# Moving the weight ring's two tiles by 32 bytes in SBUF

## The chip, the core and the metric

The kernel runs on one core of one Trainium2 chip. The metric is the device time of one execution in microseconds (us), the median of several runs. TensorE has two clock levels, 1.2 and 2.4 GHz; in the stretches used below the granted clock is 1.00 of the higher one.

## What is computed

Two transformer blocks of two layers each, all in float32, on a batch of one. The first runs over 16 meta tokens and 256 tokens (272 columns in the kernel), the second over the 256 tokens alone. Cut to what matters here:

```
# block one, twice
h = h + mixer(rms_norm(h), w_in, w_branch, w_out, ...)     # retention, hgrn2, differential attention, gates
h = h + conv_ffn(rms_norm(h), w_ffn_in, ..., w_ffn_out)    # 1024 -> 2 x 2816 -> 1024
# block two, twice
x = x + merged(rmsnorm(x) @ w_in, w_branch) @ w_out        # four branches, gated
x = x + (silu(h2 @ w_ffn_gate) * (h2 @ w_ffn_up)) @ w_ffn_down
```

Nearly all of the arithmetic is activation times weight matrix, and every weight is used once.

## The kernel before

**Products.** Activations lie feature-major: 128 features on the partitions, the tokens along the row. A weight matrix is cut into blocks of 128 x 128; a block is the stationary operand of a matmul (TensorE's weight load), the tokens (256, 258 or 272 columns) are the moving one. For float32 accuracy each operand is split into a high and a low part, and a block costs three matmuls, high x high, low x high and high x low, summed in one PSUM bank (`product`, which calls `mm`, line 468).

**The ring.** The weights come from HBM as slabs of 8 blocks (1024 columns of 4 bytes, 512 KB). The tile `ring` has 6 slots. For each slab SyncE issues one load (L2167, L2176, then L2181 in a loop that waits for `slab_used`); ScalarE copies it, rounded, into `ring_hi` (L918); VectorE (L1394), or in some stretches GpSimd (L2152), subtracts and writes `ring_lo`; TensorE multiplies and frees the slot. `ring_lo` is a twin of `ring`: the same bytes under another type, so the ring is two tiles in memory, `ring`/`ring_lo` and `ring_hi`. Each slot is 4,096 bytes long in a partition, each block 512 bytes.

**Moving operands.** The normed activations lie in `hn_hi` and `hn_lo`, 8 tiles of features each, 1,088 bytes apart in block one (272 columns) and 1,024 bytes apart in block two. Everything else that is multiplied with ring weights lies in `arena` (with its twin `arena_r`): the outputs of the branches, the summed branches (for `w_out`), the inner activations of the feed-forward part (`FF`, `FF2`, for the matrix that leads out of it, called "down") and the scaled input from which the first three products after each norm are taken.

**Where the tiles begin.** SBUF tiles are laid out one behind the other. Small tiles of 8 floats (`LINE // 2`) shift what follows by 32 bytes. The first byte of each in a partition, before:

| tile | first byte | past a multiple of 64 | past a multiple of 256 |
|---|---|---|---|
| hn_hi | 25,248 | 32 | 160 |
| hn_lo | 33,952 | 32 | 160 |
| ring, ring_lo | 42,688 | 0 | 192 |
| ring_hi | 67,264 | 0 | 192 |
| cst | 91,840 | 0 | 192 |
| arena | 114,656 | 32 | 224 |

In block two every tile of `hn_hi` and `hn_lo` is 160 past a multiple of 256, and so are their lo and hi parts alike; the operands of "down", of `w_out` and of the first three products after a norm are all 224 past one. In block one the step of 1,088 bytes makes the starts run through 32, 96, 160 and 224; where the last layer leaves out the first 14 columns (258 columns), through 24, 88, 152 and 216.

The order of the work is written out by hand in each engine's program, with semaphores; nothing in it depends on an address.

Of the kernel before, what the change touches and what calls it, by code (L numbers as in the profile page):

```python
# [114 lines left out]
LINE = 16  # L115
# [107 lines left out]
def program(nc, x_meta, w, par1, lb, lam, final1, par2, positions, final2, consts, out, known):  # L223


    with ExitStack() as ctx:
        def sb(name, n, dt=F32):
            return ctx.enter_context(nc.sbuf_tensor(name, [P, n], dt))
# [7 lines left out]
        def twin(name, n, dt):  # L236

            return nc.alloc_sbuf_tensor_at(name, [P, n], dt, offset=nc.sbuf_base - 4 * n)
# [3 lines left out]
        hn_sq = twin("hn_sq", KT * T1, F32)  # L242
        hn_lo = sb("hn_lo", KT * T1, F32R)
        hn_t = twin("hn_t", KT * T1, F32)
        sb("ring_shift", LINE // 2)
        ring = sb("ring", RING * SLAB * P)
        ring_lo = twin("ring_lo", RING * SLAB * P, F32R)
        ring_hi = sb("ring_hi", RING * SLAB * P, F32R)
        cst = sb("cst", NCONST)
        par1_sb = sb("par1_sb", DEPTH * NPAR1)  # L250
        par2_sb = sb("par2_sb", DEPTH * NPAR2)
# [2063 lines left out]
```

How the kernel before makes its waits and increments, by code:

```python
    def take(self, pe, key):  # L191
        bank, use = self.n % 8, self.n // 8 + 1
        self.n += 1
        self.known[self.stage, key] = (bank, use)
        if use > 1:
            pe.wait_ge(self.frees[bank], use - 1)
        return self.psum[:, bank, :]
# [263 lines left out]
        @block.tensor  # L461
# [12 lines left out]
            def weight_block(blocks=1):  # L474
                n = stream["n"]
                k = n // SLAB
                assert n % SLAB + blocks <= SLAB
                if n % SLAB == 0:
                    pe.wait_ge(slab_lo[k % RING], k // RING + 1)
                at = (k % RING) * SLAB * P + (n % SLAB) * P
                stream["n"] = n + blocks
                return ring_hi[:, at:at + blocks * P], ring_lo[:, at:at + blocks * P]
# [8 lines left out]
            def product(b, key, rhs, tokens, ready=None, first=0):  # L492
                ps = b.take(pe, key)
                for i, (hi, lo) in enumerate(rhs):
                    w_hi, w_lo = weight_block()
                    if ready is not None:
                        pe.wait_ge(*ready[i])
                    final = i == len(rhs) - 1
                    mm(ps[:, first:tokens], w_hi, hi[:, first:tokens], i == 0, False)
                    mm(ps[:, first:tokens], w_hi, lo[:, first:tokens], False, False)
                    mm(ps[:, first:tokens], w_lo, hi[:, first:tokens], False, final, b.filled(key) if final else None)
                    through()
                b.ended(key, stream["n"])
# [117 lines left out]
            pe.wait_ge(x_in, 16 * 3)
            for layer in range(DEPTH):
```

## Time and profile before

| | us |
|---|---|
| median of 3 runs | 2395.18 (2394.8 to 2395.27) |
| the profiled execution | 2396.62 |
| its span, first to last instruction | 2394.8 |
| TensorE busy | 2310.0 (96%) |
| VectorE busy | 1837.3 (77%) |
| ScalarE busy | 1338.2 (56%) |
| GpSimd busy | 391.4 (16%) |
| mean granted TensorE clock | 0.994 |

Busy time is time in which the engine has an instruction under way. Matmuls overlap each other in the pipeline, so a busy TensorE says little; the number that counts is how far apart their starts lie. It can be read from a stretch in which TensorE never idles: the length of the stretch plus one matmul's duration, divided by the number of matmuls that the view counts there (it counts those that began before the stretch and were still running).

### The profile page before, as it was taken

The numbers are of one execution on the slowest core, as the hardware profiler recorded it, in microseconds if no ns is written. First come the engines' busy times: TensorE is split into PE (matmuls) and PEld (weight loads), VectorE is DVE, ScalarE is ACT, GpSimd is POOL, SyncE is SP. The second block draws the span as 40 slices with busy tenths as digits, with TensorE's granted clock in tenths as the row PEclk, the third lists the DMA queues.
The fourth block names the chain that finished last, engine by engine and source line by source line (L and its number), as shares of the span: only waits on it lengthen the run. The fifth ranks groups of instructions, "written<-read, shape, count | busy, mean of one in ns | idle before, by whom it ended". The sixth has DMA issues, their size and how long they took to land.

```text
span 2394.8 us, 51593 instructions
## 1 busy us (share of the span) xinstructions
PE 2310.0 (96%) x19438; PEld 2223.1 (93%) x19438; DVE 1837.3 (77%) x3526; ACT 1338.2 (56%) x2312; POOL 391.4 (16%) x496
## 2 busy tenths in 40 slices
PE   6999999999999999999999999999999998999998
PEld 6999899899999999999889999988999998889998
DVE  6688866788886679876788887788887668888774
ACT  5655556766555565556766554655554465556443
POOL 0000002625940000001644951000000000000000
PEclk9999999999999999999999999999999999999999
DMA  5433343345555543344345555443555544445553
GB/s 201 163 125 121 107 148 122 116 147 167 175 175 171 167 142 116 115 142 132 117 141 169 177 180 172 148 144 124 176 177 185 187 165 150 133 142 185 185 185 132
DMA packets 100437, 366.68 MB, mean 153 GB/s; under 512 B 11632, under 2 KB 12144, under 8 KB 99824
## 3 DMA queue, kind: packets, MB, share of 16 engines
q1 hardware_dynamic: 100208, 363.53, 45.7%
q8 instruction: 155, 2.54, 0.4%
q14 instruction: 74, 0.61, 0.1%
HBM read 362.44 MB, written 1.05 MB: 152 GB/s over the span
## 4 chain that ended last, share of the span: by engine, by line
PE 58%; DVE 25%; DVEq 6%; ACT 5%; issue 3%; ACTq 1%; DMA 1%; SPq 0%
PE psum L468 57%; DVE ring_lo L1394 7%; DVE arena L1444 2%; ACT arena L905 2%; DVE arena_r L1382 1%; DVE arena L1436 1%; ACT ring_hi L918 1%; DVE arena_r L1380 1%; DVEq L1374 1%; DVEq L1900 1%; DVE arena L1618 1%; DVE arena L1615 1%; DVEq L1927 1%; ACT hn_hi L905 1%; DVE arena L1452 1%
## 5 line engine op out<-in xcount | busy, mean ns | idle before, releaser
L468 PE MATMUL psum<-hn_hi,ring_hi 128*128 128x272 f32 (+2 forms) x3744 | 1096.0, 293 | 40.5 <-DVE ring_lo L1394 31.3
L468 PE MATMUL psum<-hn_hi,ring_lo 128*128 128x272 f32 (+2 forms) x3744 | 1067.1, 285 | 0.0
L468 PE MATMUL psum<-hn_lo,ring_hi 128*128 128x272 f32 (+2 forms) x3744 | 1066.0, 285 | 0.0
L918 ACT ACTIVATE ring_hi<-ring 128x1024 fp32r<-128x1024 f32 x684 | 714.5, 1056 | 191.1 <-DMA ring<-w 161.4
L1394 DVE TENSOR_TENSOR ring_lo<-ring,ring_hi 128x1024 fp32r<-128x1024 f32 x564 | 689.5, 1232 | 170.7 <-ACT ring_hi L918 133.7
L468 PEld LDWEIGHTS psum<-hn_hi,ring_hi 128*128 128x128 f32 x3744 | 708.0, 189 | 67.5 <-issue 34.2
L468 PEld LDWEIGHTS psum<-hn_lo,ring_hi 128*128 128x128 f32 x3744 | 709.1, 189 | 1.6
L468 PEld LDWEIGHTS psum<-hn_hi,ring_lo 128*128 128x128 f32 x3744 | 708.1, 189 | 0.0
L468 PE MATMUL psum<-arena_r,ring_hi 128*128 128x256 f32 (+2 forms) x3380 | 621.9, 285 | 18.5 <-DVE ring_lo L1394 16.1
L905 ACT ACTIVATE arena<-psum 128x272 f32<-128x272 f32 (+8 forms) x736 | 257.1, 366 | 571.9 <-PE psum L468 490.0
L2152 POOL TENSOR_TENSOR ring_lo<-ring,ring_hi 128x256 fp32r<-128x256 f32 x480 | 381.5, 830 | 1022.4 <-ACT ring_hi L918 1022.0
L468 PEld LDWEIGHTS psum<-arena_r,ring_hi 128*128 128x128 f32 x3380 | 523.4, 189 | 22.8 <-issue 14.5
L468 PE MATMUL psum<-arena_r,ring_lo 128*128 128x256 f32 (+2 forms) x1690 | 478.2, 283 | 0.0
L468 PEld LDWEIGHTS psum<-arena_r,ring_lo 128*128 128x128 f32 x1690 | 318.9, 189 | 0.0
L468 PE MATMUL psum<-arena 128*64 128x64 f32 (+13 forms) x2464 | 185.3, 257 | 7.9 <-DVE arena L1528 6.5
L468 PEld LDWEIGHTS psum<-arena 128*64 128x64 f32 (+7 forms) x2464 | 141.7, 146 | 49.5 <-issue 14.6
L905 ACT ACTIVATE arena<-arena 128x128 f32<-128x128 f32 (+5 forms) x218 | 99.9, 503 | 126.6 <-DVEq L1374 122.1
L1382 DVE TENSOR_TENSOR arena_r<-arena,arena_r 128x256 fp32r<-128x256 f32 (+3 forms) x148 | 81.2, 549 | 11.7 <-issue 0.8
L905 ACT ACTIVATE arena<-arena,small 128x128 f32<-128x128 f32 (+1 forms) x128 | 59.3, 464 | 37.6 <-DVEq L1374 33.9
L468 PE MATMUL psum<-arena,cst 128*128 128x272 f32 (+2 forms) x232 | 69.7, 396 | 5.9 <-ACTq L1339 3.8
L1380 DVE CAST arena_r<-arena 128x256 fp32r<-128x256 f32 (+3 forms) x148 | 61.7, 417 | 12.6 <-issue 1.3
L905 ACT ACTIVATE arena<-psum,par_sb 128x272 f32<-128x272 f32 (+1 forms) x88 | 49.5, 564 | 35.7 <-PE psum L468 29.9
(174 smaller groups left out, 1480.8 us busy)
## 6 DMA issues: line engine op xcount, KB each, us to landing
ring<-w SPq DMA_DIRECT2D x684, 512.0 KB, 3.3
cst<-consts SPq DMA_DIRECT2D x1, 1960.0 KB, 13.2
x_sb<-x_meta SPq DMA_DIRECT2D x1, 1088.0 KB, 4.9
out<-x_sb SPq DMA_DIRECT2D x1, 1024.0 KB, 3.9
arena<-lam SPq DMA_DIRECT2D x1, 256.0 KB, 5.9
par_sb<-par SPq DMA_DIRECT2D x1, 193.0 KB, 5.4
pos_sb<-positions SPq DMA_DIRECT2D x1, 128.0 KB, 7.0
cst<-consts SPq DMA_DIRECT2D x1, 66.0 KB, 4.9
```

What stands on the lines that cost most here:

```text
L468: i = nc.tensor.matmul(out_, lhsT=lhsT, rhs=rhs, start=first, stop=last)
L905: i = nc.scalar.activation(out_, in_, func, **kw)
L918: nc.scalar.activation(ring_hi[:, slot], ring[:, slot], ACT.Copy).then_inc(slab_hi[k % RING], 1)
L1374: i = V.drain()
L1380: V.tensor_copy(hi, src)
L1382: return V.tensor_tensor(lo, src, hi.bitcast(F32), ALU.subtract)
L1394: V.tensor_tensor(ring_lo[:, slot], ring[:, slot], ring_hi[:, slot].bitcast(F32), ALU.subtract)\
L1436: V.tensor_tensor(zq[:, z, 0:n].rearrange("p (b t s) -> p b t s", t=2, s=s), paired(C, s, n // (2 * s), step + s), paired(C, s, n // (2 * ...
L1444: V.tensor_tensor(d, d, paired(k, s, n // (2 * s), step + s), ALU.mult)
L1452: V.tensor_tensor(Lt[:, :, :], ps[:, 0:7 * HALF].rearrange("p (a b) -> p a b", b=HALF), lvl[:, :, :], ALU.mult)
L1615: V.scalar_tensor_tensor(dst[:, t0() + 1:T1], ps[:, t0():T1 - 1], par("cw", 2 * FT + f), dst[:, t0() + 1:T1], ALU.mult, ALU.add)
L2152: i = nc.gpsimd.tensor_tensor(ring_lo[:, part], ring[:, part], ring_hi[:, part].bitcast(F32), ALU.subtract)
```

## The change

The 32-byte tile that stood ahead of the ring stands behind it. `ring`/`ring_lo` now begin at byte 42,656 and `ring_hi` at 67,232, both 32 past a multiple of 64 and 160 past a multiple of 256. Every other tile keeps its place. No instruction is added, removed or moved: on every engine the order is the same row for row.

```
         hn_t = twin("hn_t", KT * T1, F32)
-        sb("ring_shift", LINE // 2)
         ring = sb("ring", RING * SLAB * P)
         ring_lo = twin("ring_lo", RING * SLAB * P, F32R)
         ring_hi = sb("ring_hi", RING * SLAB * P, F32R)
+        sb("rest_shift", LINE // 2)
         cst = sb("cst", NCONST)
```

## Rows read from the trace of the kernel before

**Rows 1.** The chain that ended last, by engine and by line, from the page.
```profile
PE 58%; DVE 25%; DVEq 6%; ACT 5%; issue 3%; ACTq 1%; DMA 1%; SPq 0%
```

**Rows 2.** The chain in order of time: start us, length us, line, instructions; longest pieces.
```profile
315.42 92.79 PE psum L468 x688
595.45 220.65 PE psum L468 x1756
1049.17 89.60 PE psum L468 x688
1766.56 164.31 PE psum L468 x1393
2214.49 169.44 PE psum L468 x1437
```

**Rows 3.** Stretches: from:to, length, PE busy (matmuls), PE clock, DMA share, GB/s.
```profile
610.00:680.00 70.00, 70.00 (x561) 1.00 0.53 177
...
1435.00:1480.00 45.00, 45.00 (x381) 1.00 0.57 184
1780.00:1850.00 70.00, 70.00 (x594) 1.00 0.57 187
1875.00:1925.00 50.00, 50.00 (x431) 1.00 0.57 188
```

**Rows 4.** Groups by line and shape, from 1435 to 1480: count | busy us, mean ns.
```profile
L468 PE MATMUL psum<-arena_r,ring_hi 128*128 128x256 f32 x254 | 45.4, 282 | 0.0
L468 PE MATMUL psum<-arena_r,ring_lo 128*128 128x256 f32 x127 | 35.7, 281 | 0.0
```

**Rows 5.** The same view from 1780 to 1850, products from hn.
```profile
L468 PE MATMUL psum<-hn_lo,ring_hi 128*128 128x256 f32 x198 | 55.6, 281 | 0.0
L468 PE MATMUL psum<-hn_hi,ring_hi 128*128 128x256 f32 x198 | 55.6, 281 | 0.0
L468 PE MATMUL psum<-hn_hi,ring_lo 128*128 128x256 f32 x198 | 55.6, 281 | 0.0
```

**Rows 6.** The same view from 1875 to 1925, the product "down".
```profile
L468 PE MATMUL psum<-arena_r,ring_hi 128*128 128x256 f32 x287 | 50.3, 279 | 0.0
L468 PE MATMUL psum<-arena_r,ring_lo 128*128 128x256 f32 x144 | 40.1, 279 | 0.0
```

**Rows 7.** Groups by line and shape, whole span: the feeders of the ring, ended waits behind.
```profile
L918 ACT ACTIVATE ring_hi<-ring 128x1024 fp32r<-128x1024 f32 x684 | 714.5, 1056 | 191.1 <-DMA ring<-w 161.4 <-issue 0.4
...
L1394 DVE TENSOR_TENSOR ring_lo<-ring,ring_hi 128x1024 fp32r<-128x1024 f32 x564 | 689.5, 1232 | 170.7 <-ACT ring_hi L918 133.7 <-issue 6.6
...
L2152 POOL TENSOR_TENSOR ring_lo<-ring,ring_hi 128x256 fp32r<-128x256 f32 x480 | 381.5, 830 | 1022.4 <-ACT ring_hi L918 1022.0
```

**Rows 8.** The same view: instructions whose tiles begin 32 past a multiple of 64.
```profile
L905 ACT ACTIVATE hn_hi<-hn_t 128x256 fp32r<-128x256 f32 x32 | 12.9, 418 | 7.2 <-DVE hn_t L1412 7.2
...
L1419 DVE TENSOR_TENSOR hn_lo<-hn_t,hn_hi 128x272 fp32r<-128x272 f32 x32 | 11.6, 437 | 0.4
...
L1419 DVE TENSOR_TENSOR hn_lo<-hn_t,hn_hi 128x256 fp32r<-128x256 f32 x32 | 11.1, 420 | 0.4
```

**Rows 9.** GpSimd alone: squares that read x_sb and write hn_sq, 32 past a multiple.
```profile
L2147 POOL TENSOR_TENSOR hn_sq<-x_sb 128x272 f32<-128x272 f32 x4 | 2.8, 736 | 6.7 <-DMA par_sb<-par 6.7
```

**Rows 10.** DMA issues, from the page: count, KB each, median us to landing.
```profile
ring<-w SPq DMA_DIRECT2D x684, 512.0 KB, 3.3
```

**Rows 11.** Waits of SyncE's queue: in total us, times, longest us.
```profile
SPq L2181 <- PE psum L468: 1988.6, 675, 8.7
```

**Rows 12.** Waits of TensorE: in total us, times, longest us.
```profile
PE psum L468 <- DVE ring_lo L1394: 47.3, 36, 12.7
...
PE psum L468 <- POOL ring_lo L2152: 1.9, 2, 1.2
```

More of the change, by code:

```diff
@@ L244, in program @@
         hn_t = twin("hn_t", KT * T1, F32)
-        sb("ring_shift", LINE // 2)
         ring = sb("ring", RING * SLAB * P)
@@ L248, in program @@
         ring_hi = sb("ring_hi", RING * SLAB * P, F32R)
+        sb("rest_shift", LINE // 2)
         cst = sb("cst", NCONST)
```

## The prediction

> **What bounds the kernel now.** I read the chain that ended last first. TensorE holds 58% of it and VectorE 25% [rows 1], and its longest pieces are unbroken runs of ring matmuls, 220.65 us for 1,756 of them in one case [rows 2]. The reader should see that in these runs nothing is waited for: time is the number of matmuls times the distance between two starts. The rest of the chain runs through VectorE's and ScalarE's work in the recurrences, where a slightly quicker or slower matmul is absorbed. Waits of TensorE for a weight slab come to 47.3 us for VectorE's low parts and 1.9 us for GpSimd's [rows 12].
>
> So the next view is the distance between starts, in stretches with nothing but one kind of matmul. The window's length plus one duration, over the count:
>
> - products from hn with 272 columns (610 to 680): 70.29 us / 561 = 125.3 ns. 272 columns at 2.4 GHz are 113.3 ns, so 12.0 ns are on top.
> - products from hn with 256 columns (1780 to 1850): 70.28 / 594 = 118.3 ns, 11.7 on top of 106.7.
> - "down" of block two, 256 columns (1875 to 1925): 50.28 / 431 = 116.7 ns, 10.0 on top.
> - "down" of block one's last layer, 256 columns (1435 to 1480): 45.28 / 381 = 118.8 ns, 12.2 on top.
>
> These come from [rows 3], with the shapes and durations in [rows 4 to 6]. The clock is 1.00 in all four. The last three have the same shape, the same weights' place, the same two kinds of weight tile; in none does TensorE idle. What differs is where the moving operand begins: 160 past a multiple of 256 in the second, always 224 in the third, 32, 96, 160 and 224 in turn in the fourth. **So the start-to-start distance depends on addresses, by up to 2.2 ns a matmul**, and this is the only lever that the change can have.
>
> A rule of the Trainium skill speaks against that lever. "SBUF — State Buffer", in the section on the DMA port swizzle, says that SBUF has 16-byte cachelines and that what costs is crossing from one to the next. A shift by 32 bytes leaves every operand at the same place within its line, so by the rule the sum is zero and the time stays at 2395.18 us. The trace doesn't bear the rule out as the whole truth: the second and the third stretch differ by 64 bytes in start, four whole lines, and by 1.7 ns a matmul.
>
> **The change part by part.**
>
> *Loads.* 684 loads write the ring at the new place. One lands in a median 3.3 us [rows 10]. It is issued as soon as TensorE frees a slot, for which the queue waited 1988.6 us in all [rows 11], and five other slabs of 24 matmuls each (5 x 24 x 0.118 = 14.2 us) are used before the slot's turn comes. Load, high part and low part take 3.3 + 1.06 + 1.23 = 5.6 us [rows 7, 10]. A load of double length would still be in time. Cost taken: 0. If that cover were gone, each 0.1 us of landing would cost up to 0.1 us per slab.
>
> *High and low parts.* ScalarE's and VectorE's feeding instructions read and write the ring. Tiles at +32 are already in the trace: VectorE's subtraction in hn takes 437 ns for 272 columns and 420 for 256, which is 1.06 ns a column; from 420 ns at 256 columns to 1,232 at 1,024 in the ring, which begins on a multiple of 64, it is again 1.06 [rows 7, 8]. ScalarE: 418 to 1,056 ns, 0.83 a column, on one line with the engine's cost elsewhere. GpSimd's only store to a +32 tile takes 736 ns for 272 columns against 830 for 256 in the ring [rows 7, 9], so no dearer. Cost of all three: 0, since the same slope holds at either place.
>
> *Matmuls.* The weight load of the next matmul runs beside the current one, and both read SBUF. I take the distance between the two addresses as what counts: weights minus moving, past a multiple of 256. It is 192 - 160 = 32 in the second stretch, 192 - 224 = -32 in the third, and 32, 96, 160 and -32 in turn in block one. The change lowers each by 32. No row shows the new distances, so each is bounded by its neighbours on either side:
>
> - Block two from hn: 32 becomes 0, half way between 32 (1.7 ns above the cheapest) and -32 (0 above). Bounds -1.7 and 0 ns; I take the middle, -0.83. On the chain are 41 feed-forward products of 24 matmuls in each of two layers and some 200 more per layer in the merges, 2,400: -2.0 us (bounds -4.1 and 0).
> - Block two's "down", `w_out` and first products after a norm: -32 becomes -64, between -32 (0) and the mixed case (2.2). Bounds 0 and +2.2, the middle +1.1. Per layer (176 + 64) x 3 + 2 x 72 = 864, so 1,700 nearly all on the chain: +1.9 us (bounds 0 and +3.7).
> - Block one: 32, 96, 160, -32 become 0, 64, 128, -64 in turn. The mixed cases cost 2.0 to 2.2 ns above the cheapest. If cost goes smoothly with distance, the mean over one set of four equals that over the other: 0. There is no reason that forbids a step either way. About half of the extra, 1 ns, is my bound; the chain holds 0.575 x 2394.8 = 1,377 us of matmuls, some 11,000, of which 7,000 are left here: 0, with bounds -7 and +7 us.
>
> The sum is -2.0 + 1.9 + 0 = -0.1 us. Against the profiled execution (span 2394.8, time 2396.62, which lies 1.4 us above the median of the runs) that is 2396.5; against the median, **2395.1 us**.
>
> **Rivals.**
>
> *Slower: the streams fall into step.* Now nearly every ring matmul reads its moving operand from 32 past a multiple of 64 while the next weights come from a multiple of 64. After the change both cross such a boundary at the same moment. If equal phase makes them collide, every matmul on the chain pays. For it: the distances do matter, and this is the one thing the change does to all of them alike. Against it: hn at distance 32 is in opposite phase and still pays 1.7 ns, so opposite phase is no guarantee of a cheap one. Price: 1.0 ns on 11,000 matmuls is +11 us, 2406 us; if all rose by 1.7 and "down" by 2.2, +19 us. It decides from 0.44 ns a matmul on (4.8 us).
>
> *Faster: equal places suit the two reads.* hn at distance 0 falls to the cheapest 10.0 ns on top (-4.1 us) and block one's mean falls by 1 ns (-7 us): -11 us, 2384 us. For it: ring and hn share their place past 256 for the first time, and -32 is cheap while 32 isn't, so lowering a distance has helped once. Against it: nothing in the rows shows a distance of 0.
>
> *The change does nothing.* That the tiles don't move is excluded by the addresses. That the cost doesn't depend on the weights' place, only on the moving operand's, is possible: then all distances stay as they are, with 2395.2 us. It ends in the same cell as my forecast and I can't part the two beforehand. The Trainium skill's rule on 16-byte lines, named above, leads to this case as well.
>
> **How the numbers follow.** A measurement of this kernel can tell about 0.2% from no change, 4.8 us. Within it: 0.41, of which 0.25 is the cancelling sum and 0.16 the case without effect. Faster: 0.32, the second rival and those ends of my bounds in which hn gains its 4.1 us and block one adds to it. Slower: 0.27, the first rival. Predicted is the likeliest, 2395.1. The range has to reach into both rivals: up to their worked prices, 2384 and 2406, widened by a microsecond, 2383 to 2407; beyond lie the whole of the first rival's upper price and twice the second's, together under 0.2. The likeliest case's own range is 2390 to 2400.
>
> **What would show it.** In the changed profile the same four stretches, at nearly the same times, give everything: 256 columns from hn at 117.5 ns (118.3 now; 116.7 if the faster rival holds, 119 or more if the slower), "down" of block two at 117.8 (116.7 now), 272 columns at 125.3 as now (124.3 or 126.3 in the rivals). The feeders should keep 1,056 and 1,232 ns and the loads 3.3 us. I am wrong in mechanism if hn and "down" both stay at 118.3 and 116.7: then only the moving operand's place counts. I am wrong in the sum if block one's stretches move by more than 0.4 ns, since that is where most matmuls are and where I argued from smoothness alone. And if the time moves while the four distances don't, the cause is a load or a feeder, which would show as longer waits of TensorE for low parts than 47.3 us.

## The result and the profile after

The changed kernel takes 2401.73 us (median of 10 runs) against 2395.0 us beside it: the ratio is 1.0032, with a 95% interval of 1.0023 to 1.004. It is slower by 0.3%, 6.7 us, where no change was forecast. The time lies inside the range (2383 to 2407), 6.6 us above the forecast of 2395.1 and 4.3 us below the price of the rival that was called slower (2406). The profiled execution's span went from 2394.8 to 2401.2 us.

The same view of stretches as in [rows 3], of the changed kernel. Columns: from:to, length, TensorE busy and its matmuls, granted clock, DMA share, GB/s.

```profile
610.00:680.00 70.00, 70.00 (x557) 1.00 0.54 175
1435.00:1480.00 45.00, 45.00 (x384) 1.00 0.57 187
1780.00:1850.00 70.00, 70.00 (x586) 1.00 0.57 184
1885.00:1930.00 45.00, 45.00 (x384) 1.00 0.56 188
```

The groups by line and shape in the third and in the fourth of them, answering [rows 5] and [rows 6]:

```profile
L468 PE MATMUL psum<-hn_lo,ring_hi 128*128 128x256 f32 x196 | 55.5, 283 | 0.0
L468 PE MATMUL psum<-hn_hi,ring_lo 128*128 128x256 f32 x195 | 55.2, 283 | 0.0
L468 PE MATMUL psum<-hn_hi,ring_hi 128*128 128x256 f32 x195 | 55.2, 283 | 0.0
...
L468 PE MATMUL psum<-arena_r,ring_hi 128*128 128x256 f32 x256 | 45.4, 280 | 0.0
L468 PE MATMUL psum<-arena_r,ring_lo 128*128 128x256 f32 x128 | 35.7, 279 | 0.0
```

The fourth stretch, in the kernel before:

```profile
1885.00:1930.00 45.00, 45.00 (x389) 1.00 0.57 190
```

Length plus one duration, over the count: from hn, 256 columns, 70.28 / 586 = 119.9 ns (118.3 before); "down" of block two 45.28 / 384 = 117.9 (116.7 in [rows 3], 45.28 / 389 = 116.4 in this shorter stretch); 272 columns 70.29 / 557 = 126.2 (125.3); "down" of block one's last layer 45.28 / 384 = 117.9 (118.8). One matmul more or less in a count moves such a figure by 0.2 to 0.35 ns; the expectations below put the same stretches within 0.2 ns of these figures. Nothing idles and the clock is the same 1.00, so the matmuls themselves stand farther apart.

The chain in order of time (start, length, line, instructions), its runs of ring matmuls, answering [rows 2]:

```profile
314.70 93.25 PE psum L468 x688
595.86 222.09 PE psum L468 x1756
1051.08 89.43 PE psum L468 x688
...
2218.76 171.53 PE psum L468 x1437
```

With the same counts as before they grew from 92.79 to 93.25, from 220.65 to 222.09 and from 169.44 to 171.53 us; the third, with 258 columns, shrank from 89.60 to 89.43. The last alone holds 2.1 of the 6.4 us by which the span grew.

Everything beside TensorE stands still. The feeders by line and shape, answering [rows 7], the ring's load, answering [rows 10], and TensorE's wait for low parts, answering [rows 12]:

```profile
L918 ACT ACTIVATE ring_hi<-ring 128x1024 fp32r<-128x1024 f32 x684 | 712.7, 1055 | 177.4 <-DMA ring<-w 147.5 <-issue 0.4
L1394 DVE TENSOR_TENSOR ring_lo<-ring,ring_hi 128x1024 fp32r<-128x1024 f32 x564 | 689.7, 1232 | 166.3 <-ACT ring_hi L918 128.9 <-issue 6.6
L2152 POOL TENSOR_TENSOR ring_lo<-ring,ring_hi 128x256 fp32r<-128x256 f32 x480 | 381.6, 832 | 1024.3 <-ACT ring_hi L918 1023.9
...
ring<-w SPq DMA_DIRECT2D x684, 512.0 KB, 3.3
...
PE psum L468 <- DVE ring_lo L1394: 47.2, 35, 12.3
```

1,055, 1,232 and 832 ns against 1,056, 1,232 and 830; 3.3 us as before; 47.2 us of waiting against 47.3.

### The profile page after: what moved, and what is told of

The parts are those of the page before. It is cut to its first block, busy times and chain, and to the rows that moved or that the text cites. A ratio compares the mean times of both kernels' runs of the same rounds, so it can differ in the third digit from the quotient of the medians.

```text
span 2401.2 us, 51593 instructions
## 1 busy us (share of the span) xinstructions
PE 2317.3 (97%) x19438; PEld 2232.0 (93%) x19438; DVE 1836.7 (76%) x3526; ACT 1337.1 (56%) x2312; POOL 391.5 (16%) x496
## 4 chain that ended last, share of the span: by engine, by line
PE 59%; DVE 25%; DVEq 6%; ACT 5%; issue 3%; ACTq 1%; DMA 0%; SPq 0%
PE psum L468 58%; DVE ring_lo L1394 7%; DVE arena L1444 2%; ACT arena L905 2%; DVE arena_r L1382 1%; DVE arena L1436 1%; ACT ring_hi L918 1%; DVE arena_r L1380 1%; DVEq L1374 1%; DVEq L1900 1%; DVE arena L1618 1%; DVE arena L1615 1%; DVEq L1927 1%; ACT hn_hi L905 1%; DVE arena L1452 1%
## 5 line engine op out<-in xcount | busy, mean ns | idle before, releaser
L468 PE MATMUL psum<-hn_hi,ring_hi 128*128 128x272 f32 (+2 forms) x3744 | 1098.3, 293 | 41.0 <-DVE ring_lo L1394 31.8
L468 PE MATMUL psum<-hn_hi,ring_lo 128*128 128x272 f32 (+2 forms) x3744 | 1070.5, 286 | 0.0
L468 PE MATMUL psum<-hn_lo,ring_hi 128*128 128x272 f32 (+2 forms) x3744 | 1069.6, 286 | 0.0
L1394 DVE TENSOR_TENSOR ring_lo<-ring,ring_hi 128x1024 fp32r<-128x1024 f32 x564 | 689.7, 1232 | 166.3 <-ACT ring_hi L918 128.9
L918 ACT ACTIVATE ring_hi<-ring 128x1024 fp32r<-128x1024 f32 x684 | 712.7, 1055 | 177.4 <-DMA ring<-w 147.5
L468 PEld LDWEIGHTS psum<-hn_hi,ring_hi 128*128 128x128 f32 x3744 | 711.5, 190 | 67.5 <-issue 32.8
L468 PEld LDWEIGHTS psum<-hn_lo,ring_hi 128*128 128x128 f32 x3744 | 712.2, 190 | 1.6
L468 PEld LDWEIGHTS psum<-hn_hi,ring_lo 128*128 128x128 f32 x3744 | 711.7, 190 | 0.0
L468 PE MATMUL psum<-arena_r,ring_hi 128*128 128x256 f32 (+2 forms) x3380 | 624.7, 285 | 17.9 <-DVE ring_lo L1394 15.4
L468 PEld LDWEIGHTS psum<-arena_r,ring_hi 128*128 128x128 f32 x3380 | 523.9, 189 | 21.8 <-issue 13.5
L468 PE MATMUL psum<-arena_r,ring_lo 128*128 128x256 f32 (+2 forms) x1690 | 478.3, 283 | 0.0
L468 PEld LDWEIGHTS psum<-arena_r,ring_lo 128*128 128x128 f32 x1690 | 318.6, 189 | 0.0
L468 PE MATMUL psum<-arena 128*64 128x64 f32 (+13 forms) x2464 | 184.8, 257 | 7.3 <-DVE arena L1528 6.1
L468 PEld LDWEIGHTS psum<-arena 128*64 128x64 f32 (+7 forms) x2464 | 141.6, 146 | 48.7 <-issue 14.5
L468 PE MATMUL psum<-arena,cst 128*128 128x272 f32 (+2 forms) x232 | 69.9, 397 | 5.5 <-ACTq L1339 3.8
```

The source lines that it names most:

```text
L468: i = nc.tensor.matmul(out_, lhsT=lhsT, rhs=rhs, start=first, stop=last)
L918: nc.scalar.activation(ring_hi[:, slot], ring[:, slot], ACT.Copy).then_inc(slab_hi[k % RING], 1)
L1394: V.tensor_tensor(ring_lo[:, slot], ring[:, slot], ring_hi[:, slot].bitcast(F32), ALU.subtract)\
```

## The experiments

The theory under test: what counts is the **distance**, the weights' first byte minus the moving operand's, past a multiple of 256. Before it is 32 from hn and -32 from arena in block two; changed, 0 and -64. Two rivals: the **boundary** theory (weight blocks that begin 32 past a multiple of 64 cost by themselves), and the theory that only the **moving** operand's place counts. Each kernel computes all of the reference; only places in SBUF differ.

### Everything 32 bytes later

```
-        sb("hn_shift", LINE // 2)
+        sb("hn_shift", 16)
```

> Everything from hn on lies 32 bytes later: the ring is 32 past a multiple of 64, as in the changed kernel, but hn and arena have moved with it, so weights minus moving operand is 32 and -32 past 256 again, as before. Distance theory (only the distance between the two addresses that TensorE reads side by side counts): starts of 256-column products 118.3 ns apart from hn and 116.7 in block two's down, 272 columns 125.3, time 2395 us. Boundary theory (weight blocks that begin 32 past a multiple of 64 straddle nine stretches of 64 bytes instead of eight, and that costs by itself): 119.8, 117.8 and 126.1 ns as in the changed kernel, 2402 us.

Measured 2394.52 us, ratio 0.9999 (0.9989 to 1.0008). The stretches 610 to 680, 1780 to 1850 and 1885 to 1930:

```profile
610.00:680.00 70.00, 70.00 (x561) 1.00 0.53 174
...
1780.00:1850.00 70.00, 70.00 (x594) 1.00 0.55 187
1885.00:1930.00 45.00, 45.00 (x389) 1.00 0.58 188
```

125.3, 118.3 and 116.4 ns. "Down" has the count that it has in the kernel before, 389. The ring lies 32 past a multiple of 64, as in the changed kernel, and costs nothing. The boundary theory is out: where the ring lies doesn't matter while hn and arena move with it.

### hn moved down with the ring

```
-        sb("hn_shift", LINE // 2)
         hn_hi = sb("hn_hi", KT * T1, F32R)
...
+        sb("rest_shift", 8)
```

> The changed kernel with hn moved 32 bytes down as well (128 past 256), ring at 160 and arena at 224 as changed. Distance from hn is 32 again, from arena it stays -64. Distance theory: 256 columns from hn 118.3 ns, down of block two stays at 117.8, 272 columns 125.3 from hn and 126.1 from arena; some 1.5 ns x 2,400 and 0.8 ns x 4,000 come back, 2395 us. Boundary theory: nothing comes back, 119.8 and 117.8 ns, 2402 us.

Measured 2396.67 us, ratio 1.0009 (1.0 to 1.0019); the price expected was 2395. The stretches 610 to 680, 1780 to 1850, 1885 to 1930, 2330 to 2370:

```profile
610.00:680.00 70.00, 70.00 (x561) 1.00 0.52 176
...
1780.00:1850.00 70.00, 70.00 (x594) 1.00 0.57 188
1885.00:1930.00 45.00, 45.00 (x385) 1.00 0.56 187
...
2330.00:2370.00 40.00, 40.00 (x356) 1.00 0.57 185
```

From hn 125.3 and 118.3 ns again, "down" at 117.6 as in the changed kernel: the ring lies where the change put it, and hn's loss is gone because hn's distance is 32 again. The last row was not expected: the same "down", in the other layer, at the same addresses, ran at 40.28 / 356 = 113.1 ns.

### hn 64 bytes up, the ring left where it was past 256

```
-        sb("hn_shift", LINE // 2)
+        sb("hn_shift", 24)
...
-        sb("ring_shift", LINE // 2)
+        sb("ring_shift", 56)
```

> The kernel before with hn 64 bytes later, at 224 past 256, where arena lies; ring and arena keep their places past 256 (both 256 bytes on). Distance theory: 256-column products from hn fall from 118.3 to the 116.7 ns of down, down stays, block one's distances are the same set in another order and stay at 125.3; 1.65 ns x 2,400 = 4 us saved, 2391 us. Boundary theory: no start has changed its place past 64, so nothing changes, 118.3 ns and 2395 us.

Measured 2391.28 us, ratio 0.9986 (0.9977 to 0.9996). The stretch 1780 to 1850:

```profile
1780.00:1850.00 70.00, 70.00 (x602) 1.00 0.56 189
```

70.28 / 602 = 116.7 ns, as expected, and 3.3 us saved of the 4 expected.

### Only ring and ring_lo moved

```
-        sb("ring_shift", LINE // 2)
         ring = sb("ring", RING * SLAB * P)
         ring_lo = twin("ring_lo", RING * SLAB * P, F32R)
+        sb("mid_shift", 8)
         ring_hi = sb("ring_hi", RING * SLAB * P, F32R)
```

> One part of the change alone: ring and its twin ring_lo move down by 32 bytes, ring_hi stays. One weight load in three (the low part) has the new distance. Both theories: a third of the rise, 256 columns from hn 118.8 ns, down 117.0, 2397 us. If the rise came from the place that the loads from HBM are written to (ring), all of it would stand, 2402 us; if from ring_hi's place for ScalarE, none.

Measured 2393.94 us, ratio 0.9998 (0.9988 to 1.0007). The stretches 1780 to 1850 and 1885 to 1930:

```profile
1780.00:1850.00 70.00, 70.00 (x597) 1.00 0.56 186
1885.00:1930.00 45.00, 45.00 (x385) 1.00 0.58 184
```

117.7 and 117.6 ns. The loads from HBM write `ring` at its new place and nothing is lost, so the place that they write to is out. The time alone would fit the other rival named above, that `ring_hi`'s place for ScalarE makes the rise; it is out by the kernel with hn moved down, where `ring_hi` lies where the change put it and hn's loss is gone, and by ScalarE's 1,055 ns in the changed kernel. But a third of the rise was a miss, in the time too (2397 expected): from hn it is cheaper than either pure case (118.3 and 119.9), and "down" has all of its rise. With mixed distances the cost isn't the mean of the parts.

### A sweep of the ring's place

hn at 160 and arena at 224 past 256 in all four; the ring at 224, 0, 32 and 128. The edit, for the first:

```
-        sb("ring_shift", LINE // 2)
+        sb("ring_shift", 16)
...
+        sb("rest_shift", 56)
```

> Sweep of the ring's place with hn fixed at 160 past 256 and arena at 224: the ring at 224, so the distance (weights minus moving, past 256) is 64 from hn and 0 from arena. So far 256-column starts lay 117.8 ns apart at -64, 116.7 at -32, 120.0 at 0, 118.3 at 32. One curve for both sources: down of block two 120.0 ns. If the curve repeats every 128 bytes: from hn at 64 as at -64, 117.8. Block one's set of distances is 0, 64, 128, 192 as in the changed kernel: 272 columns 126.1. Time about 2402 us. Theory that the curve belongs to the tile and not to the distance: down keeps 117.8.

> The ring at 0 past 256: distance 96 from hn, 32 from arena. One curve: down of block two 118.3 ns, as hn had at 32. If it repeats every 128 bytes: from hn 116.7, as at -32; if only every 256, open. Block one's set is 32, 96, 160, 224 as before: 272 columns 125.3. Time about 2394 us.

> The ring at 32 past 256: distance 128 from hn, 64 from arena. Repeating every 128 bytes: from hn 120.0 ns as at 0, down 117.8 as at -64, 272 columns 126.1, time about 2402 us. Repeating every 256: both open, between 116.7 and 121.

> The ring at 128 past 256: distance -32 from hn, -96 from arena. One curve: from hn 116.7 ns. Repeating every 128 bytes: down as at 32, 118.3; 272 columns 125.3; about 2394 us.

One execution each: 2392.99, 2395.04, 2398.53 and 2394.86 us, beside 2395.73 of before. The stretches 1780 to 1850 (from hn) and 1885 to 1930 ("down"), ring at 224, then 0, then 32, then 128:

```profile
1780.00:1850.00 70.00, 70.00 (x620) 1.00 0.57 196
1885.00:1930.00 45.00, 45.00 (x378) 1.00 0.53 182
```

```profile
1780.00:1850.00 70.00, 70.00 (x599) 1.00 0.54 187
1885.00:1930.00 45.00, 45.00 (x382) 1.00 0.55 188
```

```profile
1780.00:1850.00 70.00, 70.00 (x592) 1.00 0.55 183
1885.00:1930.00 45.00, 45.00 (x399) 1.00 0.57 190
```

```profile
1780.00:1850.00 70.00, 70.00 (x602) 1.00 0.56 189
1885.00:1930.00 45.00, 45.00 (x378) 1.00 0.53 182
```

The figures for 256 columns by distance, those of the two kernels of the next section included (length plus duration, over count):

| distance | from hn, ns | "down" of block two, ns |
|---|---|---|
| -96 | | 119.8 |
| -64 | | 117.9 (changed kernel), 113.1 in one place of another |
| -32 | 116.7 (twice) | 116.7 (before) |
| 0 | 119.9 (changed kernel) | 119.8 |
| 32 | 118.3 (before) | 118.5 |
| 64 | 113.4; 117.7 in one layer of each kernel of the next section | 113.5; 117.9 and 113.1 in the next section |
| 96 | 117.3 | |
| 128 | 118.7 | |

At the four distances from -32 to 64 both sources have a value and agree within 0.3 ns (at 64 on the same two levels), though the tiles differ: "down" at 0 was expected at 120.0 and at 32 at 118.3 from hn's figures alone. A curve that repeats every 128 bytes is out: 119.8 at -96 stands against 118.3 at 32, and 118.7 at 128 against 119.9 at 0. So the expected values that rested on it were missed: from hn 117.8 at 64, 116.7 at 96 and 120.0 at 128, "down" 118.3 at -96 and 117.8 at 64. Two times were missed with them: 2402 expected and 2392.99 measured for the first, where hn fell to 113.4, and 2402 against 2398.53 for the third, where "down" did.

### Distance 64 for hn, with arena at 64 or at -32

The first kernel (hn and arena at 224, ring at 32), and the second (before, with hn 32 bytes lower):

```
-        sb("hn_shift", LINE // 2)
+        sb("hn_shift", 24)
...
-        sb("ring_shift", LINE // 2)
+        sb("ring_shift", 16)
...
+        sb("rest_shift", 40)
```

```
-        sb("hn_shift", LINE // 2)
...
-        sb("ring_shift", LINE // 2)
+        sb("ring_shift", LINE)
```

> hn and arena both at 224 past 256 and the ring at 32, so the distance is 64 from hn and from arena alike. At 64 the hn products ran at 113.3 ns in the sweep, and at 64 or -64 down ran at 113.4 in one place and 117.8 in another. Distance theory: 256 columns from hn 113.3 ns, down 113.4 or 117.8; block one's set is 0, 64, 128, 192, so 272 columns at 126.1. Against before: -5.0 ns x 2,400 = -12 us from hn, -3.3 x 1,700 = -5.6 or +1.9 us from down, +0.8 x 5,000 = +4 us from block one: 2381 or 2389 us. Theory that only the moving operand's place counts: hn and down as in the kernel with hn at 224, 116.7, time 2391 us.

> The kernel before with hn 32 bytes lower, at 128 past 256; ring 192 and arena 224 as before. Distance 64 from hn, -32 from arena. Distance theory: 256 columns from hn 113.3 ns, down 116.7, 272 columns 126.1 from hn and 125.3 from arena: -12 + 0.8 x 3,300 = -9 us, 2386 us. Moving-place theory: hn had 118.3 at 128 past 256 in the kernel where the ring was at 160, so 118.3 and 2395 us.

Measured: 2386.02 us, ratio 0.9964 (0.995 to 0.9978), and 2387.24 us, ratio 0.9967 (0.9955 to 0.998). Both beat the kernel before, and the changed one, which took 2402.98 us beside them. The first kernel's products from hn in its two layers (1780 to 1850, 2225 to 2305), then the second's:

```profile
1780.00:1850.00 70.00, 70.00 (x597) 1.00 0.57 188
...
2225.00:2305.00 80.00, 80.00 (x708) 1.00 0.60 196
```

```profile
1780.00:1850.00 70.00, 70.00 (x620) 1.00 0.59 196
...
2225.00:2305.00 80.00, 80.00 (x682) 1.00 0.56 188
```

117.7 and 113.4 ns; 113.4 and 117.7 ns. At distance 64 the same addresses and the same instructions have two levels, and one or the other holds for a whole stretch. That would account for the first one's median between its two prices and for its spread from 2379.91 to 2396.2 us over ten runs; only one of the ten was traced, so it isn't shown. The theory of the moving operand's place is out: it wanted 116.7 and 118.3.

### Is a level fixed?

> The changed kernel once more, one look. If a stretch's pitch is fixed by addresses: 120.0, 117.8 and 126.1 ns in the same places again. If the same addresses have two levels and chance picks one: down at 113.3 ns in some place.

> The kernel with hn and ring both 32 bytes down once more, one look. Its last down ran at 113.3 ns where the one before, with the same addresses, ran at 117.8. Fixed by addresses and order: 117.8 and then 113.3 again. Two levels, taken by chance: another pattern.

The changed kernel, again at 2402.98 us: its stretches 1780 to 1850, 1885 to 1930 and 2330 to 2370 count 586, 384 and 342 matmuls, just as before. The other, at 2397.08 us, in the stretches 1885 to 1930 and 2330 to 2370:

```profile
1885.00:1930.00 45.00, 45.00 (x384) 1.00 0.56 187
...
2330.00:2370.00 40.00, 40.00 (x342) 1.00 0.58 186
```

Now both "down" ran at 117.8 to 117.9 ns; the 113.1 is gone. So at -64 the level isn't set by the addresses, nor by the program. The two executions ran on different chips, but the chip doesn't settle it either: the level changes within one execution. In the kernel with hn and arena both at distance 64, three stretches of the second layer (products from arena ahead of a norm; from arena and then hn behind it; from hn alone) and, in time between the last two, TensorE's first matmul after a wait (this kernel has one line more, so its L469 and L1395 are L468 and L1394 of the kernel before):

```profile
2170.00:2190.00 20.00, 20.00 (x179) 1.00 0.58 189
2195.00:2208.00 13.00, 13.00 (x113) 1.00 0.64 216
2225.00:2305.00 80.00, 80.00 (x708) 1.00 0.60 196
```

```profile
2209.39 0.38 PE L469 MATMUL psum<-hn_hi,ring_hi 128*128 128x256 f32 x1 [0.53 <-DVE ring_lo L1395]
```

20.28 / 179 = 113.3, 13.28 / 113 = 117.5 and 80.28 / 708 = 113.4 ns. Ahead of the wait of 0.53 us for a low part and behind it the source is hn, with the same addresses past 256, and the level is another. By the start times of block two in the fourteen traces, no unbroken run of 20 or more ring matmuls from one source changes its level on the way, and the short products from hn show both levels in all three kernels where hn is at 64. So in these traces a level is taken at the start of an unbroken run and held to its end; what decides it there is open.

## Why the prediction was wrong, point by point

**What bounds the kernel, and the lever: right.** The matmuls' starts moved apart, while the feeders' durations, the landing and TensorE's wait for low parts stayed.

**Loads and feeders at zero: right**, by the rows above and by the kernel in which only `ring` and `ring_lo` moved.

**From hn, 32 to 0: the step that failed.** It took the middle between the neighbours, -0.83 ns, with bounds of -1.7 and 0. It measured +1.6 (118.3 to 119.9), outside both. Distance 0 is dearer than its neighbours on either side. The bounds assumed that cost changes evenly from -32 to 32, and nothing in the rows said so. On the prediction's 2,400 matmuls that is +3.9 us instead of -2.0, a miss of 5.9 us in this term, where the forecast missed by 6.6 in all (2401.7 against 2395.1). With the 2.0 and the 1.7 us of the next two points the terms add up to 7.6 us against 6.7 measured, so the split is an estimate, good to about a microsecond.

**"Down", -32 to -64: right.** +1.2 ns (116.7 to 117.9) against +1.1, 2.0 us against 1.9. The value was right by luck, since the same interpolation failed next to it, and its upper bound was no neighbour at all but the mixed case of block one.

**Block one, taken at zero: missed within its bounds.** By the prediction's own sign, a move of more than 0.4 ns in block one's stretches, this term was wrong too. 272 columns went from 125.3 to 126.2 ns, and 126.2 or so stood in every kernel whose distances from hn are multiples of 64 for both kinds of weight tile (557 or 558 matmuls in 70 us against 561 or 562). With 256 columns ("down" of the last layer) it fell by 0.9, and the 258-column run of the chain by 0.2 us. The mean over one set of four isn't that over the other. The three block-one runs of the chain shown above changed by +0.46, +1.44 and -0.17 us, +1.7 of the 7 allowed for.

**The rivals.** The slower one gave 2406 us and came nearest, and its place was right in one respect: distance 0, which the change gave hn for the first time, is among the dearest. Its mechanism was not: it made every matmul pay for sharing a boundary phase of 64 bytes, but distances that are multiples of 64 hold the cheapest values of all (113.4 at 64) as well as 119.9 at 0, and block one's 256-column stretch got cheaper. The faster rival was wrong at the place where it put its gain, hn at 0. The case without effect, that only the moving operand's place counts, fell with the result itself: hn and arena stayed where they were and both pitches rose.

**The page's rule.** The Trainium skill, "SBUF — State Buffer", in its section on the DMA port swizzle, counts crossings of 16-byte lines, by which a shift of 32 bytes changes nothing. By that rule the changed kernel, the one with hn 64 bytes up and the one with the ring at 224 would all have kept 118.3 ns from hn. They gave 119.9, 116.7 and 113.4.

**What is shown and what is argued.** Shown, for 256 columns: the distance between the two operands sets the pitch, at 64 and -64 to one of two levels; moving both together by 32 bytes changes nothing; and the place where the ring's writers write has no part in it. Argued only: that the reason is the next weight load reading SBUF beside the moving operand. That the distance counts past a multiple of 256 is an assumption: past multiples of 512 the block-two distances of all the kernels lie between 0 and 224 (-32 is 224, -64 is 192, -96 is 160), so none of them tells a curve that repeats every 256 bytes from one that repeats every 512. What picks a level at the start of a run at 64 and -64 is open, and so is how the costs combine where the distances alternate, as in block one and in the kernel with `ring_lo` alone moved. Shifts of less than 32 bytes weren't tried.

## What to carry to other kernels

Where TensorE is the bound, count starts in an unbroken stretch of equal matmuls: if two such stretches with the same columns differ, the operands' addresses are a lever. Judge an alignment change by the distance between the weights and the moving operand, not by either tile's own boundary, and move one tile at a time over all multiples of 32 up to 256 instead of guessing between two known points. At a distance with two levels take several executions before you judge. Two sources that share one weight ring have each their own distance, so their tiles can be placed apart.

## What the runs showed of the hardware

- With 256 columns and fp32r operands of 128 x 128, at a granted clock of 1.00, starts lie 113.1 to 119.9 ns apart by placement alone, 6.4 to 13.2 ns over the 106.7 that 256 columns make at 2.4 GHz.
- The curve isn't smooth: 119.8 ns at -96, 113.1 or 117.9 at -64, 116.7 at -32, 119.9 at 0, 118.3 at 32, 113.4 or 117.7 at 64, 117.3 at 96, 118.7 at 128.
- At distances of 64 and -64 an unbroken stretch holds one of two levels, 113.4 or 117.8 ns. The next stretch after a wait can hold the other (113.3, 117.5 and 113.4 ns in one execution), and so can the same stretch in another execution (113.1 and 117.8 ns).
- With 272 columns whose starts run through four places past 256, at a granted clock of 1.00, the two sets of distances gave 125.3 and 126.2 ns.
